# One Trainium2 core, four layers in float32: the narrow first product turned round, two weight tiles at a time behind each norm, the weight splits beside the residual sums taken off GpSimd, and the program's first norm and the mixers' evictions reordered

## What is computed

```python
def rms_norm(x, gain):                     # 8 times: norms n0 to n7
    return x * rsqrt(mean(x * x) + eps) * gain

# block 1
h = rms_norm(x, norm_mix[0])
proj = h @ w_in                            # q, k, v, z, and 32 columns b, a
beta, g = sigmoid(b), -exp(a_log) * softplus(a + dt_bias)
x = x + (gated_delta_rule(conv(q, k, v), beta, g) * silu(z)) @ w_out
x = x + swiglu(rms_norm(x, norm_ffn[0]), w_gate_up[0], w_down[0])
x = x + mla_mixer(rms_norm(x, norm_mix[1]))
x = x + swiglu(rms_norm(x, norm_ffn[1]), w_gate_up[1], w_down[1])
x = rms_norm(x, final_norm)
# block 2, l = 0, 1
sh1, sc1, g1, sh2, sc2, g2 = split(silu(c) @ ada_w[l] + ada_b[l], 6)
h = rms_norm(x, norm1[l]) * (1 + sc1) + sh1
x = x + g1 * (concat(four mixers of h @ w_in[l]) @ w_out[l])
h = rms_norm(x, norm2[l]) * (1 + sc2) + sh2
x = x + g2 * conv_glu_ffn(h)
```

## Time and profile before

| | us |
|---|---|
| median of three runs | 1665.9 |
| the profiled execution: its own time | 1660.92 |
| its span, first to last instruction | 1659.0 |
| PE busy / DVE / ACT / POOL | 1549.5 / 1074.0 / 888.8 / 417.1 |

### The profile page before, as it was taken

The page is one execution under the profiler, slowest core; times in us unless marked ns, Lnnn a source line. Parts: engine busy times, 40 slices in busy tenths (PEclk is TensorE's granted clock), DMA queues, the critical chain, the costliest instruction groups (busy, mean ns, idle before and its releaser), DMA issues.

```text
span 1659.0 us, 35254 instructions
## 1 busy us (share of the span) xinstructions
PE 1549.5 (93%) x15256; PEld 1407.0 (85%) x15256; DVE 1074.0 (65%) x1782; ACT 888.8 (54%) x1456; POOL 417.1 (25%) x283
## 2 busy tenths in 40 slices
PE   7999998899999979999989889899998889989999
PEld 6888988779998867999878777799987778789987
DVE  3664464457779676677976666676746665676664
ACT  5654563455443555644456555566635664566652
POOL 1343362233434100344321320112301221012220
PEclk9999999999999999999989989899999996999999
DMA  6332210548889442788943202555451400445550
GB/s 242 138 103 79 79 52 25 209 144 323 313 327 366 139 178 77 289 322 323 359 154 120 83 29 80 225 178 178 168 175 60 144 27 28 188 154 170 191 186 26
DMA packets 40042, 275.88 MB, mean 166 GB/s; under 512 B 4560, under 2 KB 4688, under 8 KB 8528
## 3 DMA queue, kind: packets, MB, share of 16 engines
q1 hardware_dynamic: 39888, 273.63, 45.1%
HBM read 272.57 MB, written 1.05 MB: 165 GB/s over the span
## 4 chain that ended last, share of the span: by engine, by line
PE 81%; DVE 8%; ACT 6%; issue 2%; DMA 1%; POOL 1%; SPq 0%; ACTq 0%; POOLq 0%; DVEq 0%
PE ps L547 23%; PE ps L548 22%; PE ps L549 22%; PE ps L555 3%; PE ps L560 2%; DVE wl L535 1%; ACT wh L527 1%; DMA ring<-in_ws 1%; PE ps L2146 1%; DVE x_sb L2959 1%; DVE hTl L687 1%; PE ps L924 1%; POOL hTl L693 0%; ACT ps L734 0%; DMA cst<-in_cst 0%
## 5 line engine op out<-in xcount | busy, mean ns | idle before, releaser
L535 DVE TENSOR_TENSOR wl<-ring,wh 128x1024 fp32r<-128x1024 f32 (+3 forms) x364 | 459.0, 1266 | 342.8 <-ACT wh L527 341.8
L527 ACT ACTIVATE wh<-ring 128x1024 fp32r<-128x1024 f32 (+4 forms) x428 | 437.4, 1028 | 447.6 <-PE ps L549 439.4
L547 PE MATMUL ps<-hTh,wh 128*128 128x256 f32 x1904 | 553.2, 291 | 5.8 <-POOL hTl L693 3.0
L549 PE MATMUL ps<-hTh,wl 128*128 128x256 f32 x1904 | 544.7, 286 | 1.6 <-issue 1.6
L548 PE MATMUL ps<-hTl,wh 128*128 128x256 f32 x1904 | 543.4, 285 | 0.0
L547 PEld LDWEIGHTS ps<-hTh,wh 128*128 128x128 f32 x1904 | 367.0, 193 | 15.6 <-issue 13.8
L548 PEld LDWEIGHTS ps<-hTl,wh 128*128 128x128 f32 x1904 | 366.8, 193 | 0.2
L549 PEld LDWEIGHTS ps<-hTh,wl 128*128 128x128 f32 x1904 | 364.5, 191 | 0.0
L543 POOL TENSOR_TENSOR wl<-ring,wh 128x1024 fp32r<-128x1024 f32 x64 | 170.2, 2659 | 608.6 <-ACT wh L527 608.6
L1449 DVE SCALAR_TENSOR_TENSOR arena<-arena 128x1024 f32<-128x1024 f32 x96 | 158.0, 1663 | 1.0 <-DMA arena<-in_ws 1.0
L547 PE MATMUL ps<-wh,acts 128*128 128x512 f32 x366 | 145.2, 397 | 0.8 <-DVE wl L535 0.8
(11 more groups left out here) (464 smaller groups left out, 2152.0 us busy)
## 6 DMA issues: line engine op xcount, KB each, us to landing
ring<-in_ws SPq DMA_DIRECT2D x197, 1024.0 KB, 5.0
arena<-in_ws SPq DMA_DIRECT2D x48, 1024.0 KB, 8.2
ring<-in_ws SPq DMA_DIRECT2D x5, 768.0 KB, 4.5
ring<-in_ws SPq DMA_DIRECT2D x4, 512.0 KB, 3.6
ring<-in_ws SPq DMA_DIRECT2D x2, 780.0 KB, 4.2
rowt<-in_rowp SPq DMA_DIRECT2D x2, 610.0 KB, 4.1
x_sb<-in_x SPq DMA_DIRECT2D x2, 512.0 KB, 4.1
arena<-in_rowp SPq DMA_DIRECT2D x2, 512.0 KB, 4.6
```

The source lines that it names most:

```text
L527: ac.act(unit_hl(u)[0], unit_src(u), ACT.Copy).then_inc(*W.a(("hi", u)))
L535: ve.tt(l, unit_src(u), h, OP.subtract).then_inc(*W.v(("lo", u)))
L547: pe.mm(o_, lh, rh, start=start, stop=False)
L549: return pe.mm(o_, ll, rh, start=False, stop=stop)
```

## The change

- `ba_t` uses `tile_T`: the 32 columns are stationary and 256 tokens move, 24 products with an output of 32x256. Two transposes and two copies (`bav`) bring the result back to tokens. ACT and DVE split `ba` ahead of the first norm's k, and the next unit between k = 3 and k = 4.
- The identity is loaded by a DMA of its own between the two halves of x. The row table, the rest of the constants and the positions are issued after the first three ring loads. A square root of a constant at the start loads ACT's table for n0 before x arrives.
- At the six norms in front of tiles of `tile_T` (n1, n3 to n7) `two_T` issues tiles 0 and 2 together, k by k, into two banks; tile 1 comes next. For this, units 1 and 2 change places, and so their loads' lists.
- At n1 to n7 the unit U+1 is no longer POOL's. Its ACT half stays where it was. DVE's half ("late") stands behind the second scaling of x and ahead of the first k.
- In block 2 the copies of the blocks stand 1.1 positions earlier (`pjo`), and the dot products of "lam" in the product ahead of them ("dot").

```diff
+    for name in ("f0u", "f1u", "win0", "f2u", "win1", "f3u"):
+        a, b = index[name, 1], index[name, 2]
+        units[a], units[b] = units[b], units[a]
+        index[name, 1], index[name, 2] = b, a
+        la, lb = units[b].load, units[a].load
+        loads[la].units, loads[lb].units = [a - 1, b], [a, b + 1]
     for name in ("f0u", "mi0", "f1u", "win0", "f2u", "win1", "f3u"):
-        units[index[name, 1]].pool, units[index[name, 2]].pool = True, False
+        u = index[name, 0]
+        units[u + 1].pool, units[u + 2].pool, units[u + 1].late = False, False, True
...
+        def two_T(pe, u, os, kt, rh, rl, come):
+            for i in range(2):
+                pe.wait_ge(*lo_done(u + i))
+            for k in range(kt):
+                for c in come(k):
+                    pe.wait_ge(*c)
+                m = [mm3(pe, os[i], unit_hl(u + i)[0][:, k, :], unit_hl(u + i)[1][:, k, :], rh(k), rl(k), k == 0, k == kt - 1) for i in range(2)]
+            for i in range(2):
+                m[i].then_inc(*W.t(("used", u + i)))
...
         def norm_a(ac, n, at, gain, bias):
+            yield "pre"
             if n:
...
+            else:
+                ac.wait_ge(*N.v[0, "pre"])
+                ac.act(small[:, 11:12], small[:, 10:11], ACT.Sqrt).then_inc(*N.a((n, "pre")))
...
         def norm_t(pe, n, at):
                 if n == 0:
-                    pe.wait_ge(*DMA["cst"]["cst"])
+                    pe.wait_ge(*DMA["idn"]["idn"])
...
         def ba_t(pe):
-            unit_tok(pe, UIX["ba", 0], [psum[4][:, 0:32], psum[5][:, 0:32]], 0, 8, 8, h_, l_, h_come(0))
+            tile_T(pe, UIX["ba", 0], psum[4][0:32, 0:256], 8, h_, l_, h_come(0))
...
         def up_t(pe, s, n):
-                tile_T(pe, UIX[f"f{s}u", m], psum[UB[i % 4]][:, 256 * (m % 2):256 * (m % 2) + 256], 8, h_, l_, h_come(n) if m == 0 else None)
+                if m == 0:
+                    two_T(pe, UIX[f"f{s}u", 0], [psum[UB[j]][:, 0:256] for j in range(2)], 8, h_, l_, h_come(n))
+                elif m != 2:
+                    tile_T(pe, UIX[f"f{s}u", m], psum[UB[i % 4]][:, 256 * (m % 2):256 * (m % 2) + 256], 8, h_, l_)
...
         def close(tid, res, n, first):
-                    of(nt, [("mean", 1)] * (n != 4) + [("sqrt", 1), ("scale", 1), ("T", 1)]) + of(nt, [("k", k) for k in range(8)]) + [[("fill", U + 2)]])
+                    of(nt, [("mean", 1)] * (n != 4) + [("sqrt", 1), ("scale", 1)]) + [[("w", ("late", U + 1))]] + of(nt, [("T", 1)]) + of(nt, [("k", k) for k in range(8)]) + [[("fill", U + 2)]])
...
+        plan_ += [[("fill", ba0)]] + of("n0", [("k", k) for k in range(4)]) + [[("fill", ba0 + 1)]] + of("n0", [("k", k) for k in range(4, 8)]) + of("ba", [0])
...
-            plan_ += weave((0, pjs), *[(end_of[b] + 0.1, of(f"pjv{l}", [b])) for b in range(5)],
+            plan_ += weave((0, pjs), *[(end_of[b] + T0["pjo"], of(f"pjv{l}", [b])) for b in range(5)],
...
         def sync(e):
-            for t in range(2):
-                sp.dma(x3[:, t, :], xs[:, t, :]).then_inc(*DMA[f"x{t}"](t))
+            sp.dma(x3[:, 0, :], xs[:, 0, :]).then_inc(*DMA["x0"](0))
+            sp.dma(cst[:, 0:128], A["cst"][:, 0:128]).then_inc(*DMA["idn"]("idn"))
+            sp.dma(x3[:, 1, :], xs[:, 1, :]).then_inc(*DMA["x1"](1))
             sp.dma(colt[:, :], A["colp"]).then_inc(*DMA["col"]("col"))
```

More of the change, by code:

```diff
@@ L258, in __init__ @@
     def __init__(self, load, view, pool):
-        self.load, self.view, self.pool = load, view, pool
+        self.load, self.view, self.pool, self.late = load, view, pool, False
 def weight_units(offs):
@@ L417, in build_program @@
         DMA = {k: Signal(sem(f"landed_{k}"), 16) for k in
-               ("x0", "x1", "col", "cst", "row", "pos", "row_l0", "row_l1", "misc0", "misc1", "ada0", "ada1", "ada2", "cond", "out")}
+               ("x0", "x1", "idn", "col", "cst", "row", "pos", "row_l0", "row_l1", "misc0", "misc1", "ada0", "ada1", "ada2", "cond", "out")}
         RING = [Signal(sem(f"landed_ring{i}"), 16) for i in range(NSLOT)]
@@ L531, in split_v @@
                 if not UNITS[u].pool:
-                    yield u
+                    yield ("late", u) if UNITS[u].late else u
                     ve.wait_ge(*W.a["hi", u])
@@ L664, in norm_v @@
             xn = arena[:, at:at + 2048]
+            if n == 0:
+                yield "pre"
+                ve.zero(small[:, 10:11], 1.0).then_inc(*N.v((0, "pre")))
             for t in range(2):
@@ L842, in gates_t @@
             yield 3
+            pe.wait_ge(*DMA["cst"]["cst"])
             pe.wait_ge(*GP.v["g"])
@@ L1592, in krope_p @@
             yield "zero"
+            po.wait_ge(*AD.v[0, "mod"])
             po.zero(krp, 0.0).then_inc(*ML.p("krp"))
@@ L1865, in pa_t @@
                 yield m
-                tile_T(pe, UIX[f"win{l}", m], psum[4 + m // 2][:, 256 * (m % 2):256 * (m % 2) + 256], 8, h_, l_, h_come(4 + 2 * l) if m == 0 else None)
+                if m == 0:
+                    two_T(pe, UIX[f"win{l}", 0], [psum[4 + j][:, 0:256] for j in range(2)], 8, h_, l_, h_come(4 + 2 * l))
+                elif m != 2:
+                    tile_T(pe, UIX[f"win{l}", m], psum[4 + m // 2][:, 256 * (m % 2):256 * (m % 2) + 256], 8, h_, l_)
         def pa_a(ac, l):
@@ L2160, in df_v @@
             S = DF[l]
-            yield "lam"
+            yield "dot"
             ve.wait_ge(*DMA[f"row_l{l}"][0])
@@ L3172, in pump @@
                     loaded[0] += 1
+                    if loaded[0] == 3:
+                        ORDER.append(("late", "consts"))
             def fill(u):
@@ L3209, in sync @@
             xs, os_ = (ap.rearrange("(t p) n -> p t n", p=128) for ap in (A["x"], out))
-            for t in range(2):
-                sp.dma(x3[:, t, :], xs[:, t, :]).then_inc(*DMA[f"x{t}"](t))
+            sp.dma(x3[:, 0, :], xs[:, 0, :]).then_inc(*DMA["x0"](0))
+            sp.dma(cst[:, 0:128], A["cst"][:, 0:128]).then_inc(*DMA["idn"]("idn"))
+            sp.dma(x3[:, 1, :], xs[:, 1, :]).then_inc(*DMA["x1"](1))
             sp.dma(colt[:, :], A["colp"]).then_inc(*DMA["col"]("col"))
-            sp.dma(cst[:, :], A["cst"]).then_inc(*DMA["cst"]("cst"))
-            sp.dma(rowt[:, 0:1056], A["rowp"][:, 0:1056].to_broadcast([128, 1056])).then_inc(*DMA["row"]("row"))
-            sp.dma(posi[:, :], A["posi"]).then_inc(*DMA["pos"]("pos"))
-            follow(ORDER, {"ring": ring_s(sp), "adal": ada_s(sp), "rows": rows_s(sp)})
+            follow(ORDER, {"ring": ring_s(sp), "late": late_s(sp), "adal": ada_s(sp), "rows": rows_s(sp)})
             for t, n in PIECES:
```

32 lines of the change are left out of this document (22 added, 10 removed).

## The result

The changed kernel takes 1646.2 us (median of 4 runs, 1641.1 to 1650.2) against 1665.3 for the kernel before in the same comparison: ratio 0.988, 95% interval 0.9856 to 0.9904, so 19 us less and clearly faster by the bound of 0.5%. In a second comparison the ratio was 0.9909 (0.9874 to 0.9943), 1644.3 against 1661.0. The forecast was 1639.5. The profiled execution is the slowest of its four, 1650.2 with a span of 1648.4; against the profiled one before (1659.0) it gained only 10.6.

The account below looks back on a forecast made before the run. PE was taken to bound the kernel, busy 1549.5 of 1659.0 us. Start 10.2, n4 to n7 12.2, n1 to n3 0 and mixers 4 sum to 26.4, so 1665.9 becomes 1639.5; range 1628 to 1654.

Parts of the forecast that it names:

- The start: No table load, `ba` product from near 11 to 17.05, first full unit ending at 21.0 instead of 31.62: 10.6 us.
- The wait of ACT for the ring: At the start, a sign that the first full load came late; one us late would cost one us.
- 5 behind 14.5: At the start, PE's clock reaches its upper level 5 us after 14.5: 11.5 products of 0.213, then 12.5 of 0.12.
- I count 10.2 for the start: The start's term in the sum: 10.2 us, beside the 10.6 worked out for the first full unit's end.
- the last sentence of the prediction: Names signs that the prediction is wrong, among them time won at one place being gone at the end of its stage.
- Norms n4 to n7: Hole falls to 2.9, third tile starts 13.1 behind zero (PE's last work ahead of the hole): 12.2 us over four.
- 5.7 for DVE's sum alone: At n4 to n7, removing POOL's split takes DVE's second sum from 2.12 to 0.69: 1.43 a norm, 5.7 kept.
- The level never falls: Rival: PE's clock stays up at n4 to n7, gaining 18.4, and mixers keep all: 34 in all, 1632; chance 0.15.
- n1 to n3: DVE's late split delays the first k by 0.2; nothing gained at n1 and n3, at most 0.2 lost at n2.
- The mixers: Earlier copies out of PSUM shorten PE's waits ahead of blocks 3 and 4; 4 us kept in the sum.
- that is 5.0: Mixers' gain in both layers: 0.62 and 0.6 at block 3, 1.67 and 2.10 at block 4.
- The sum: Start 10.2, n4 to n7 12.2, n1 to n3 0, mixers 4: 26.4 us off the median 1665.9, giving 1639.5.

Follow-up runs that it names:

- head22: Kernel before with only the start's changes, plus 22 idle 32x32 transposes ahead of PE's first ones; gains 11.5 us by its ratio.
- after22: Changed kernel plus 22 idle 32x32 transposes ahead of PE's first ones; 1638.5 us, ratio 0.9836 to the kernel before.
- after64: Changed kernel plus 64 idle 32x32 transposes (128 instructions, half a block) ahead of PE's first ones; 1640.0 us, ratio 0.9856.
- nomix22: Changed kernel with 22 idle transposes at the start and the mixers' copies and dot products as in the kernel before; ratio 0.9858.
- head: Kernel before with only the start's changes; norms n1 to n7 and mixers as before; 1660.9 us, ratio 0.9996.
- after: The changed kernel itself, in the first comparison with the kernel before; 1646.2 us, ratio 0.988.
- again: The same changed kernel timed and traced once more, in the second comparison; 1644.3 us, ratio 0.9909.
- nomix: Changed kernel with the mixers' copies and dot products back where the kernel before had them; 1647.7 us, ratio 0.9920.
- locks: Changed kernel without two tiles at a time and the exchange of units 1 and 2; DVE's late split kept; 1652.1 us.
- after128: Changed kernel plus 128 idle 32x32 transposes (256 instructions, a whole block) ahead of PE's first ones; 1648.4 us.
- two: Changed kernel with POOL's residual splits back and two tiles at a time kept, but no late split on DVE; 1664.2 us.
- the rest alone: Changed kernel with the start's changes undone, keeping those of the norms and mixers; 12.8 us faster than the kernel before by the ratio.

## Why the prediction was right or wrong

**The start**: every step came as written or better. No table load in the way; first narrow product at 11.59 (near 11); the product done by 16.47 (17.05); full unit at 19.34 (21); 32x256 at the step of its neighbours. The wait of ACT for the ring, named as the sign of a late load, was there (2.18 at 19.92), and no wait of PE shows from 19 to 27 us. What was mis-sized up to there is the clock: the level rose some 2 us behind the first product, where I took 5 behind 14.5. "I count 10.2 for the start" failed as a term of the sum: the gain was gone at the end of its stage, as the last sentence of the prediction allowed, and alone the start gives 0.7 us (-3.3 to 4.8).

In the traces two things took it back. The first is settled: the turned product has 24 products where it had 48, PE's program is some 40 instructions shorter, and all later borders of its blocks of 256 moved. In 14 traces, between 100 and 345 us, a block's packet started 1.1 us (median of 399) behind the border that calls for it, and 3.3 us (median of 81) where a load of the ring was under way; in some other blocks it started before PE came to the border. A border shortly ahead of 64 small products, or under a load, stalls PE. With the borders moved, the four kernels with the early start reach n1 5.0, 3.6, 9.5 and 10.3 us ahead of the kernel before (head22, after22, after64, nomix22); with them left, or moved by a whole block, 2.0, -1.6, 2.3, 2.4, -1.0 and -1.6 (head, after, again, nomix, locks, after128), and -4.5 in two, whose clock column is the highest (22.2). That a load delays the packet is read off those pairs; it was not tried alone.

The second is the clock, and in these traces it is as large as the first. The stretches in which the two differ most (columns as in the earlier trace rows); the first four rows are of the kernel before, the last four of the changed one:

```profile
100.00:120.00 20.00, 18.94 (x258) 16.97 (x257) 15.83 (x37) 12.05 (x20) 8.84 (x7) 1.00 0.32 109
120.00:140.00 20.00, 18.42 (x610) 16.65 (x610) 8.08 (x11) 9.51 (x14) 4.70 (x5) 1.00 0.15 56
260.00:300.00 40.00, 30.23 (x1058) 27.91 (x1057) 13.76 (x26) 11.65 (x21) 6.45 (x6) 0.89 0.32 124
300.00:340.00 40.00, 39.25 (x480) 32.50 (x480) 16.56 (x33) 18.60 (x34) 15.75 (x13) 0.98 0.38 143
```
```profile
100.00:120.00 20.00, 19.31 (x416) 16.95 (x416) 10.52 (x18) 5.33 (x10) 3.74 (x3) 0.89 0.15 55
120.00:140.00 20.00, 17.36 (x612) 15.91 (x612) 6.85 (x15) 9.11 (x14) 6.80 (x5) 0.94 0.19 61
260.00:300.00 40.00, 30.78 (x985) 28.18 (x972) 11.81 (x23) 9.22 (x17) 6.45 (x6) 0.87 0.43 174
300.00:340.00 40.00, 36.65 (x386) 29.65 (x385) 15.16 (x30) 17.08 (x32) 14.70 (x12) 0.91 0.26 93
```

The lower level cost 8.5 us in the kernel before and 15.4 in the changed one, 6.9 more, where the waits marked issue are 6.6 more. In head22 the waits are those of the kernel before (7.4 and 7.6), and still 12.0 us of lead have become 5.0 at n1: the clock column has the rest. The three kernels with the late start lost 6.9 to 11.9, the eleven with the early one 10.2 to 22.2.

The stalls do not cause all of it. Each of the eleven has a stretch at 0.50 that begins between 115 and 123 us, ahead of its first wait marked issue over 0.25 us (126.2 at the earliest); the three others have none between 55 and 150. Whether the earlier start brings the lower clock stays open. One execution of each kernel is traced, the kernel before's stood 5.0 below its median, and over whole executions the mean granted clock was 0.956 in the twelve of head and 0.957 in the twenty of the kernel before beside them. That head22 gains 11.5 by its ratio also speaks for the borders as the larger cause in the medians.

**Norms n4 to n7**: right by the steps named: the hole from 4.36 to 2.94, no second hole, the first product at 4.9 to 5.2. That the size is 12.1 for 12.2 is in part luck, since both lean on one slow n5 of the kernel before. The four third tiles sum to 49.4 to 52.5 in the eight traces that have both parts, and to 62.9 to 67.7 in the four that have neither. By locks, 7.6 of the 12.1 come with POOL's split gone and 4.5 with two tiles; the working had 5.7 for DVE's sum alone, and 5.9 are left of the 7.6 without the slow n5. *The level never falls* did not happen: it fell at all four.

**n1 to n3**: right. The third tile of n1 and of n3 starts 9.28 behind zero where it started 9.50 behind, 0.2 less; "nothing" was forecast.

**The mixers**: "that is 5.0" was wrong, in both of its parts. For block 3 the working had the split of 128x1024 decide even with the copy ahead of it, a gain of 0.62. In the changed kernel block 3 starts at 922.95 and that split at 925.94, so block 3 never needed it: its hole shrank by 3.9. For block 4 the working took 1.67 and 2.10 as won; its copy still came behind a split, and its hole grew by 2.6 in both layers. The hole was mostly handed on, not closed.

**The sum** of 26.4 had two misses of one sign: some 10 us of start that did not arrive and most of the 4 of the mixers. What is left is 15 to 20 us by the two ratios, of which the rest alone gives 12.8. The measured 1646.2 lies in the range because the terms of the norms held and the range was wide enough for the loss of a whole term that no rival spoke of. The fastest version is the changed kernel with 22 idle transposes, 1638.5: its interval lies below that of again and touches that of the first comparison at 0.986. The versions with 64 transposes (0.9856) and with 22 and the mixers undone (0.9858) can't be told from it. That the version with 22 comes out at the forecast 1639.5 is luck in part: at n1 its trace is 3.6 us ahead where 10.2 were counted, and the mixers' 4 are not there.

## What to carry to other kernels

Where an engine runs hundreds of small products, look at its waits marked issue and count instructions to them: if they stand multiples of a fixed number apart (256 here), the engine is bound by how its program arrives, and any edit that changes the count of instructions moves the cost of stages it never touches. Before a gain of under 1% is believed or given up, try the same edit with a few dozen idle instructions in an early hole. And a wait that is moved off one block of a chain is worth only what the next block does not ask back.

## What the hardware showed that I had not expected

- In 14 traces 195 waits of PE over 0.25 us are marked issue. All end within two of instruction 193 + 256 n; they take up to 2.4 us each, 7 to 17 us per execution.
- The packet of an instruction block started 1.1 us behind its border on idle queues, 3.3 under a load of 1 MB, and PE went on 2.2 to 2.9 us behind that start.
- In all 14 traces the time from the first full unit to n1 is 318.5 to 323.0 us, plus the waits marked issue (5.2 to 14.2), plus what the lower clock cost (6.9 to 22.2).
- The level of PE's clock rose about 2 us behind the first product of the changed start (step 0.21 at 11.59, 0.12 at 13.42), where 10 us of narrow moving columns in the kernel before had left it low.
- 22 transposes of 32x32 in fp32 took 1.35 us and 106 took 5.8, 0.061 and 0.055 us each at the start, while 64 products of 32x32 in the delta stage took 0.86, 0.013 each.
